# Two-block transformer kernel: level 0 of the triangular inverse from its mask, shorter roots, fillers, later low halves

## What is computed

```python
def first_block(x, ...):
    for l in range(2):
        h = _rmsnorm(x, norm_mix[l])
        p_rw, p_sb, p_ret, p_conv = split(h @ w_in[l])
        branches = (_rwkv7_mixer(p_rw, ...), _stick_breaking_mixer(p_sb, ...),
                    _retention_mixer(p_ret, ...), _conformer_conv_mixer(p_conv, ...))
        merged = sum(sigmoid(h @ w_gate[l, i]) * (branches[i] @ w_branch[l, i]) for i in range(4))
        x = x + merged @ w_out[l]
        h = _rmsnorm(x, norm_ffn[l])
        x = x + (_swiglu(h, ...) if l == 0 else _moe_ffn(h, ...))

# _rwkv7_mixer: kk = kk32 / sqrt(sum(kk32 * kk32)), then for each position
    sa = einsum('bhvk,bhk->bhv', state, -kk_t)
    state = state * w_t + sa[..., None] * (kk_t * a_t) + v_t[..., None] * k_t
    y_t = einsum('bhvk,bhk->bhv', state, r_t)
# and: layernorm of y by head, y + sum(r * k * r_k) * v (the bonus), times g

def second_block(x, ...):
    x = ssd_dilated_layer(x, ...)
    x = moba_layer(x, ...)   # with 256 positions: causal softmax attention of 16 heads,
                             # q and k normed and turned by RoPE, output times silu(g), @ w_out
```

## Time and profile before

| | |
|---|---|
| three executions | 2007.81, 2008.08, 2009.65 us |
| profiled execution | 2006.37 us, span 2004.6 us |
| mean granted PE clock | 0.991 of full speed |
| PE, DVE, ACT, POOL busy | 96%, 64%, 46%, 6% of the span |
| chain that ended last | PE 82%, DVE 11%, ACT 3%, issue 2% |
| DMA | 321.84 MB, mean 161 GB/s |

### The profile page before, as it was taken

How to read it: one execution, slowest core, us unless ns; L and a number is a source line. 1 busy time by engine, 2 the same in 40 slices (tenths; PEclk the granted TensorE clock), 3 DMA queues, 4 the chain that set the end, 5 groups by cost and what they waited for, 6 DMA issues and landing times.

```text
span 2004.6 us, 34247 instructions
## 1 busy us (share of the span) xinstructions
PE 1923.2 (96%) x14639; PEld 1766.9 (88%) x14639; DVE 1289.0 (64%) x1835; ACT 928.4 (46%) x1110; POOL 124.3 (6%) x82
## 2 busy tenths in 40 slices
PE   7899999999998999999999999999999999889998
PEld 7789999999998899988788888888899989789978
DVE  5985566555579647655455558888887557854563
ACT  4443344433443423434444346777655443444453
POOL 0000000000000000000101010101200001100023
PEclk9999999999999999999999999999999999999999
DMA  7321245555442213545455468999999766224420
GB/s 279 106 85 54 93 171 190 175 184 189 153 148 85 67 62 132 191 168 167 160 166 177 150 219 284 326 329 327 324 178 179 135 103 129 94 65 144 129 85 22
DMA packets 235016, 321.84 MB, mean 161 GB/s; under 512 B 6257, under 2 KB 173425, under 8 KB 234609
## 3 DMA queue, kind: packets, MB, share of 16 engines
q1 hardware_dynamic: 234112, 317.76, 51.9%
q10 hardware_dynamic: 752, 1.90, 0.3%
HBM read 317.01 MB, written 1.05 MB: 159 GB/s over the span
## 4 chain that ended last, share of the span: by engine, by line
PE 82%; DVE 11%; ACT 3%; issue 2%; DMA 0%; SPq 0%; DVEq 0%; ACTq 0%
PE b L363 81%; DVE s_arena L379 4%; DVE s_ring_lo L472 2%; ACT s_wh L388 2%; PE b L1884 1%; DVE s_roots L379 1%; ACT s_arena L388 1%; DVE s_arena L2223 1%; DVE s_arena L382 0%; DMA s_ring<-w_in 0%; DVE s_arena L2145 0%; DVE s_arena L1333 0%; DVE s_roots L401 0%; ACT s_arena L385 0%; DVE s_roots L382 0%
## 5 line engine op out<-in xcount | busy, mean ns | idle before, releaser
L472 DVE TENSOR_TENSOR s_ring_lo<-s_ring,s_wh 128x2048 fp32r<-128x2048 f32 (+3 forms) x307 | 647.7, 2112 | 382.0 <-ACT s_wh L388 381.0
L388 ACT ACTIVATE s_wh<-s_ring 128x2048 fp32r<-128x2048 f32 (+3 forms) x329 | 574.3, 1747 | 270.2 <-PE b L363 264.3
L363 PE MATMUL b<-s_Hh,s_wh 128*128 128x256 f32 x1832 | 535.6, 292 | 4.8 <-DVE s_Hl L564 2.2
L363 PE MATMUL b<-s_Hl,s_wh 128*128 128x256 f32 x1832 | 522.1, 285 | 0.0
L363 PE MATMUL b<-s_Hh,s_ring_lo 128*128 128x256 f32 x1832 | 521.8, 285 | 0.0
L363 PEld LDWEIGHTS b<-s_Hh,s_wh 128*128 128x128 f32 x1832 | 354.5, 193 | 15.6 <-issue 6.1
L363 PEld LDWEIGHTS b<-s_Hl,s_wh 128*128 128x128 f32 x1832 | 354.7, 194 | 0.6
L363 PEld LDWEIGHTS b<-s_Hh,s_ring_lo 128*128 128x128 f32 x1832 | 354.5, 193 | 0.0
L363 PE MATMUL b<-s_wh,s_arena_r 128*128 128x512 f32 (+1 forms) x964 | 305.5, 389 | 3.2 <-DVE s_arena_r L2065 2.6
L363 PE MATMUL b<-s_arena_r,s_wh 128*128 128x256 f32 x1184 | 217.9, 285 | 9.6 <-ACT s_arena_r L388 5.9
L363 PEld LDWEIGHTS b<-s_wh,s_arena_r 128*128 128x128 f32 x964 | 180.4, 188 | 41.5 <-DVE s_arena_r L2065 3.9
(11 more groups left out here) (180 smaller groups left out, 1948.9 us busy)
## 6 DMA issues: line engine op xcount, KB each, us to landing
s_ring<-moe_w SPq DMA_DIRECT2D x96, 1024.0 KB, 5.2
s_ring<-moe_w SPq DMA_DIRECT2D x48, 768.0 KB, 4.4
s_ring<-ffn_w SPq DMA_DIRECT2D x33, 1024.0 KB, 4.9
s_ring<-w_gate SPq DMA_DIRECT2D x32, 1024.0 KB, 5.1
s_ring<-even_w_in SPq DMA_DIRECT2D x32, 1024.0 KB, 12.0
s_ring<-w_in SPq DMA_DIRECT2D x26, 1024.0 KB, 5.1
s_ring<-odd_w_in SPq DMA_DIRECT2D x16, 1024.0 KB, 5.3
s_ring<-w_out SPq DMA_DIRECT2D x8, 1024.0 KB, 6.6
```

Of the source, the lines that this page charges most:

```text
L363: return e.matmul(out, l, r, start=start, stop=True, skip_group_check=True)
L388: return e.activation(out, x, ACT.Copy, scale=scale)
L472: e.tensor_tensor(l_, r_, h_.bitcast(F), SUB).then_inc(*up(engine, z % "lo", i))
```

## The change

It does five things.

1. `root` has 8 operations in place of 11: one operation for the start value, one step with tuned constants, one third-order step.
2. `fill` of 11 before the first product of branch 3, of 5 before the sums of squares of the keys (the wait for "a tanh" is ahead of it now), and of 9 before the bonus sums, in each of the two mixers.
3. Level 0 of the inverse has no X and Y product and no copy of T on ACT. DVE subtracts Am itself from Ym8 and the T product, in PSUM, from Xm. DVE has three operations of 128x512 there as before.
4. `PLAN` loses one K, so that level 0 takes one slot: its T product moves one slot later, to where its X and Y products stood. All later steps keep their slots.
5. `attend_rest` moves within an iteration of `attend_dve` from first place to behind "attended".

```diff
--- before.py
+++ after.py
@@ -391,19 +391,21 @@
             return e.activation(out, x, ACT.Exp, **k)
 
         def root(e, x, y, a):
-            ts(e, y.bitcast(I32), x.bitcast(I32), 1, None, ALU.logical_shift_right).then_inc(*up("V"))
-            e.wait_ge(*now("V"))
-            ts(e, y.bitcast(I32), y.bitcast(I32), -1.0, 1597463007.0, MUL, ADD).then_inc(*up("V"))
-            for i in range(3):
-                e.wait_ge(*now("V"))
-                stt(e, a, y, -0.5, y, MUL, MUL).then_inc(*up("V"))
-                e.wait_ge(*now("V"))
-                e.tensor_tensor(a, a, x, MUL).then_inc(*up("V"))
-                e.wait_ge(*now("V"))
-                last = stt(e, y, a, 1.5, y, ADD, MUL)
-                if i < 2:
-                    last.then_inc(*up("V"))
-            return last
+            ts(e, y.bitcast(I32), x.bitcast(I32), -0.5, 1595932665.0, MUL, ADD).then_inc(*up("V"))
+            e.wait_ge(*now("V"))
+            stt(e, a, y, -0.703952253, y, MUL, MUL).then_inc(*up("V"))
+            e.wait_ge(*now("V"))
+            e.tensor_tensor(a, a, x, MUL).then_inc(*up("V"))
+            e.wait_ge(*now("V"))
+            stt(e, y, a, 0.703952253 * 2.38924456, y, ADD, MUL).then_inc(*up("V"))
+            e.wait_ge(*now("V"))
+            stt(e, a, y, 0.375 ** 0.5, y, MUL, MUL).then_inc(*up("V"))
+            e.wait_ge(*now("V"))
+            e.tensor_tensor(a, a, x, MUL).then_inc(*up("V"))
+            e.wait_ge(*now("V"))
+            stt(e, a, a, -1.25 / 0.375 ** 0.5, a, ADD, MUL).then_inc(*up("V"))
+            e.wait_ge(*now("V"))
+            return stt(e, y, a, 1.875, y, ADD, MUL)
 
         def sums(e, cols_, tiles):
             for i in range(2):
@@ -685,6 +687,8 @@
                 yield
             for f in range(4):
                 need_bank(e, l, 14 + f)
+                if f == 0:
+                    fill(e, bank_of(14), 11)
                 last = branch(3, f, f, bank_of(14 + f))
                 last.then_inc(*(up("PE", "used", li[f"b3{l}", 0]) if f == 3 else up("PE", "b3", l, f)))
                 if f % 2:
@@ -1102,14 +1106,16 @@
                 last = mm(e, b6[:, T * i:T * i + T], lg[:, 128 * i:128 * i + 128], rtmp[:, 0, :], True)
             last.then_inc(*up("PE", "lora g", l))
             yield
+            e.wait_ge(*on("a tanh", l, 1))
+            fill(e, b7, 5)
             e.wait_ge(*on("kk squares", l))
-            e.wait_ge(*on("a tanh", l, 1))
             sums(e, table(b7, 2), [rtmp[:, i, :] for i in range(2)]).then_inc(*up("PE", "kk sums", l))
             yield
             e.wait_ge(*on("kk root", l))
             e.wait_ge(*on("gg", l))
             spread(e, b6, factor_view(rt3, 2), (0, 1)).then_inc(*up("PE", "kk wide", l))
             yield
+            fill(e, b7, 9)
             e.wait_ge(*on("bonus", l))
             for i in range(2):
                 last = mm(e, b7[:, T * i:T * i + T], c("blk"), rtmp[:, i, :], True)
@@ -1148,6 +1154,8 @@
                         last = mm(e, b[hs, 64 * j:64 * j + 64], Am[hs, j, :], Xm[hs, j, :], True)
                 last.then_inc(*up("PE", "T product", l, lv))
                 yield
+                if lv == 0:
+                    continue
                 e.wait_ge(*on("T", l, lv))
                 for j in range(8):
                     for hs in HALVES:
@@ -1234,6 +1242,9 @@
             for q in range(4):
                 yield
             for lv in range(6):
+                if lv == 0:
+                    yield
+                    continue
                 e.wait_ge(*on("T product", l, lv))
                 copy(e, Tm, eight((b7, b6)[lv % 2])).then_inc(*up("A", "T", l, lv))
                 yield
@@ -1339,11 +1350,21 @@
                 yield
             for lv in range(6):
                 bx, by = (b6, b7) if lv % 2 == 0 else (b7, b6)
-                yield
+                if lv:
+                    yield
+                else:
+                    e.wait_ge(*on("eye", l))
+                    e.wait_ge(*on("level mask", l, 0))
+                    e.tensor_tensor(Ym8, Ym8, Am, SUB).then_inc(*up("V"))
+                    e.wait_ge(*now("V"))
                 if lv < 5:
                     msk = c("lvl")[:, 64 * lv + 64:64 * lv + 128].unsqueeze(1).broadcast_to([128, 8, 64])
                     e.wait_ge(*on("T product", l, lv))
                     e.tensor_tensor(Am, m3(Gm)[:, :, 0:64], msk, MUL).then_inc(*up("V", "level mask", l, lv + 1))
+                if lv == 0:
+                    e.tensor_tensor(Xm, Xm, eight(b7), SUB).then_inc(*up("V", "Y", l, 0))
+                    yield
+                    continue
                 e.wait_ge(*on("X product", l, lv))
                 e.tensor_tensor(Xm, Xm, eight(bx), SUB).then_inc(*up("V"))
                 e.wait_ge(*on("Y product", l, lv))
@@ -1392,7 +1413,7 @@
 
 
 
-        PLAN = (". .K .K .K" + " .KC" * 4 + " .KCS" * 9 + " .KS" * 5 + " .KC" * 13 + " .K" * 4 + " ." * 13).replace(" ", "")
+        PLAN = (". .K .K .K" + " .KC" * 4 + " .KCS" * 4 + " .CS" + " .KCS" * 4 + " .KS" * 5 + " .KC" * 13 + " .K" * 4 + " ." * 13).replace(" ", "")
 
         def walk(plan, reciprocals=False, **steps):
             steps["."] = steps.pop("bulk")
@@ -2207,8 +2228,6 @@
 
         def attend_dve(e, name, cases, z):
             for t in range(len(cases) + 2):
-                if t >= 3 and cases[t - 3].part is not None:
-                    attend_rest(e, name, cases[t - 3])
                 if t < len(cases):
                     case, m = cases[t], z.m[t % 2]
                     e.wait_ge(*on("scores", name, t))
@@ -2230,6 +2249,8 @@
                         o = o.rearrange("p (a m) -> p a m", a=2)
                     e.wait_ge(*on("out", li["og", (t - 2) // 2] if name == "oo" else li["eg", (t - 2) // 4]))
                     stt(e, case.out, o, 0.5, case.gate, MUL, MUL).then_inc(*up("V", "attended", name, t - 2))
+                if t >= 3 and cases[t - 3].part is not None:
+                    attend_rest(e, name, cases[t - 3])
                 yield
                 if t < len(cases):
                     m = z.m[t % 2]
```

## The result

The changed kernel takes 1989.84 us (median of four, 1989.28 to 1991.70), the kernel before 2008.25 (median of four): 18.4 us less, a ratio of 0.9908 with a 95% interval of 0.9893 to 0.9924. The forecast was 1995.2 with a range of 1990 to 2002.

What follows compares the result with a forecast made beforehand. PE, busy 96% of the span, was taken as the bound, except DVE near each mixer's start. Roots -5.2, level 0 -0.6, rest -4.1 and clock -3 made -12.9 from 2008.1: 1995.2 us, range 1990 to 2002.

Steps and rivals of the forecast that it cites:

- Roots: Norms, key norm and stick branch: three fewer dependent DVE operations save up to 0.6 us per root, -5.2 in all.
- The other nine I cost at nothing: Remaining nine roots: DVE or PE waits longer than 0.6 us on another product, so 0, bounds 0 and -5.4.
- After 0.41 the filler is the longer one: Four norms behind 18 filler products of 2.17 us: only PE's gap of 0.41 can be won, 4 x -0.4 = -1.6.
- Fillers: Three added fills in each mixer: 12.0 us of PE work in all, lying in idle time, so 0.
- Level 0: Inverse in each mixer: PE products fall away, but DVE's convolution products limit the win to -0.3 each, -0.6 in all.
- Rest of a pair: Odd layer's attend_rest: moved past POOL's piece, it takes 0.69 instead of 2.75 us, twice -2.06, -4.1.
- Clock: Three half-clock stretches behind gaps the change touches should go: bounds 0 and -5.1 us, taken as -3.
- The rest still meets POOL: Rival: the moved attend_rest still overlaps POOL, 4.1 us and one clock drop's share stay, 2000 to 2002 us; chance 0.12.
- nothing: Rival: DVE has another wait behind each root and a new one behind the moved rest, 2008 us; chance 0.04.
- slower: Rival: PE's own queue bounds the mixers' start and every filler is paid, +2.1, 2010.2 us; chance 0.03.
- Clock unchanged: Rival: half-clock drops come from elsewhere or move, leaving only -9.9, 1998.2 us; chance 0.2.
- level 0 is worth its full PE time: Rival: PE, not DVE, bounds 115 to 150 us, 2 x 2.08 in place of 0.6, 1991.6 us; chance 0.1.

Runs made afterwards that it cites:

- f2: The kernel before with only attend_rest moved behind the gated output: 2001.75 us, 6.2 less than the kernel before.
- g1: The changed kernel run again unaltered, on one chip with its variants: 1989.42 us, 19.2 less than the kernel before.
- f3: The kernel before with only the three added fills (11, 5 and 9) in each mixer: 2005.75 us, 2.2 less than the kernel before.
- h3: The changed kernel without its added fillers: 1993.02 us, 15.1 less than the kernel before.
- f4: The kernel before with only the change to level 0 of the inverse and the shorter PLAN: 2009.57 us, 1.6 more than the kernel before.
- g2: The changed kernel with its edits on level 0 and PLAN undone: 1989.50 us, 19.2 less than the kernel before.
- h4: The changed kernel with level 0's T product left in its old slot, X and Y products still gone: 1990.58 us, 17.6 less than the kernel before.
- h2: The changed kernel with DVE's level 0 operations reordered and fillers in two more gaps (8 and 9): 1988.75 us, 19.4 less than the kernel before.
- group f: The single-part kernels, each one part of the change in the kernel before, with their own 24 runs of the kernel before: median 2007.94 us.

## Why the prediction was right and wrong

**Roots.** Right about the ten roots that were priced. Wrong by 1.2 in the sum (-5.2 forecast, -6.4 measured), in two places. "The other nine I cost at nothing" failed for two of them, one head norm's root in each mixer, worth 0.19 and 0.18. And "After 0.41 the filler is the longer one" took the 2.17 us of a row for the time that 18 fillers hold PE. They hold it for 2.01, so the four norms gave 0.6 each: 0.8 more.

**Fillers.** Right: none of the 12.0 us is paid, the one doubtful place included (1.09 before the bonus sums; the wait behind it stays 2.45).

**Level 0.** The bound was the right one (DVE's convolution products), and the value, -0.3 a mixer, was too good: -0.05 to -0.1. Two things were left out. PE follows DVE by 0.14 at the least, so only 0.19 of the 0.33 was to be had, and "so DVE gains and loses nothing" passed over the wait that the new operation puts in front of the mask, 0.12. Nor did the prediction follow where the gap went that the T product had filled: by 1.1 us longer, to 2.0. And it has nothing of the 0.26 at 290.42. With it the whole part comes to some -0.4 for the -0.6 forecast, which is closer than the reasoning deserved: over half of it lies where the prediction did not look.

**Rest of a pair.** Right to 0.05 us: -4.13 for -4.1, and by the rows f2 gives the same. The reading of the Trainium skill ("SBUF — State Buffer", section "SBUF: two separate sides") under which the masks would be held up by POOL is contradicted by the row at 1927.38; the rule itself, that an operation with two SBUF inputs is held, fits the rest's 2.75 beside POOL and 0.68 without.

**Clock.** This is the step that failed. The parts without it come to -6.4 - 4.1 - 0.5 = -11.0 (0.5 are level 0 and the 0.05 a mixer that the fillers give in front of branch 3), against -9.9 forecast. Measured is -18.4, so the clock gave 7 to 8 and not 3. The three drops that were priced did all go, and the ledger has -1.46, -1.35 and -1.56 for them, 4.4 in all where the bound said 5.1; the remainder came from drops elsewhere. I took "bounds 0 and -5.1" from three half-clock stretches that stood behind gaps the change touches, and held the other eight of that trace for fixed. They are not. g1 and the first profile of the change are one kernel with different drops. So a single trace cannot say which drops a change removes, and the mean over runs is the thing to forecast: 0.989 before and 0.994 to 0.995 after. 0.001 of mean clock over a span of 2000 us is 2 us of full-speed work, a little more than one stretch of 3.4 us at half clock (1.7 of work lost; about 1.5 of time where PE bounds, 0.6 behind the stick branch's product, 0 to 0.12 where DVE bounds). 0.0055 is then 6 to 7 such stretches fewer, up to 10 us and less where DVE bounds, and 7 to 8 are to be explained.

Which part raised the clock was measured, part by part: roots +0.002, rest +0.001, fillers +0.003, level 0 nothing; together +0.006, and the change has +0.0055. The fillers' share is shown twice, by f3 and by h3. The +0.001 of the rest is no more than the spread of its seven runs allows (0.987 to 0.992). In time, the four parts alone add up to -15.6 by their medians. The change has -18 to -19; with the spread of single runs (2 to 8 us within one kernel) the 3 between them are not settled; h3 shows the fillers worth 3 to 4 us inside the change, and 2.2 alone. That roots and rest raise the clock because they shorten gaps of 1.6 to 3.1 us is argued from what they do, not shown: no run shortened the gaps and nothing else, except the fillers.

**The rivals.** "The rest still meets POOL", "nothing" and "slower" did not come. "Clock unchanged" is out by the clocks of all runs of the change (0.994 to 0.997, against 0.986 to 0.991). That level 0 is worth its full PE time is out by f4, g2 and h4. The best of the tried versions, h2, is not told apart from the change by its time.

## What to carry to other kernels

Where a gap of PE is followed by half clock in a trace, count all such stretches of the program, not those next to the edit, and forecast the mean clock over several runs; shortening or filling many gaps of 1 to 3 us may be worth as much as the waits themselves. Ask of every stretch which engine bounds it before pricing PE's work or PE's clock in it: in the mixers' first part and around the convolution products DVE does, and there PE's work cost nothing, and 3.4 us at half clock cost 0 to 0.12 in the one and 0.6 in the other, in place of 1.5. And when an instruction leaves a slot, look at the gap it leaves behind, and at the operation that now overwrites what its neighbour has just read.

## What the runs showed of the hardware

The mean granted clock of single executions of one kernel differed, from 0.986 to 0.991 over the 24 runs of the kernel before in group f, and the time followed it: the five runs at 0.991 took 2006.6 to 2007.4 us, the four at 0.986 and 0.987 took 2009.5 to 2012.9. The same gap may be followed by half clock in one execution and by full clock in another (2.00 at 113.81 and 2.00 at 113.35, above).

And half clock does not need a gap. Ahead of the stretch at 1605.40 in the trace of before the profile shows no idle time of PE, but its work was of short products, here the last of them and the stretch that holds them:

```profile
1602.38 0.69 PE L363 MATMUL b<-s_arena,s_c 16*128 16x256 f32 x2
1603.01 0.86 PE L363 MATMUL b<-s_arena 128*64 128x256 f32 x4
1603.80 1.05 PE L363 MATMUL b<-s_c,s_arena 128*128 128x1 f32 x8
...
1602.00:1605.40 3.40, 3.40 (x25) 2.73 (x24) 2.81 (x5) 1.94 (x4) 0.00 (x0) 1.00 0.71 120
```

The busy share of PE hides this: 3.40 of 3.40 us.

A row that groups many short matmuls overstates by some 0.15 us how long they hold PE: 2.17 by the row, 2.01 by the start of what follows.
